# Projection and modulation units issued in four parts instead of two, in a hybrid recurrent decoder step

## The reference

```python
hmix = (_rms(x, p['norm1_w']) * (1 + sc1) + sh1)
proj = (h @ p['w_in']).astype(jnp.float32)          # q, k, v, gates of four mixers
# A gated DeltaNet, B HGRN2, C Mamba-2 SSD, D mLSTM, each 256 wide, recurrent in chunks
up = jnp.einsum('btnw,nwd->btnd', branches, p['w_branch'])
merged = jnp.einsum('btnd,btnd->btd', gates, up)
x = x + gt1 * (merged @ p['w_out'])
x = x + gt2 * _swiglu(hffn, p['ffn_w_in'], p['ffn_w_out'])
```

## Time and profile before

| | before |
|---|---|
| median of 3 runs | 1434.14 us (1432.4 to 1435.74) |
| the profiled execution | 1436.71 us, its span 1434.9 us |
| TensorE matmul busy | 1337.7 us, 93% of the span |
| VectorE busy | 633.8 us, 44% |
| ScalarE busy | 382.3 us, 27% |
| mean granted TensorE clock | 0.96 |

### The profile page before, as it was taken

The page is one execution under the profiler, slowest core; times in us unless marked ns, Lnnn a source line. Parts: engine busy times, 40 slices in busy tenths (PEclk is TensorE's granted clock), DMA queues, the critical chain, the costliest instruction groups (busy, mean ns, idle before and its releaser), DMA issues. The chain is left out here.

```text
span 1434.9 us, 23172 instructions
## 1 busy us (share of the span) xinstructions
PE 1337.7 (93%) x9801; PEld 1159.4 (81%) x9801; DVE 633.8 (44%) x1240; ACT 382.3 (27%) x561; POOL 11.7 (1%) x29
## 2 busy tenths in 40 slices
PE   6789989988999999999899999996999999989997
PEld 3368857767767676758899999896999999989996
DVE  1142663357677777463433333545322222263332
ACT  1231271173222121114521212112322222251112
POOL 0000110000000000000000000000000000000000
PEclk9889999999999999869999999998999999999999
DMA  8701703222202020305463332222233333223301
GB/s 293 219 3 59 150 12 100 68 89 89 86 4 89 1 89 1 90 0 130 49 187 98 93 84 93 74 59 60 59 88 88 88 88 88 60 60 91 88 26 63
DMA packets 191019, 116.77 MB, mean 81 GB/s; under 512 B 36650, under 2 KB 189351, under 8 KB 190678
## 3 DMA queue, kind: packets, MB, share of 16 engines
q1 hardware_dynamic: 190358, 115.41, 29.0%
q0 software_dynamic: 576, 0.14, 0.1%
HBM read 108.57 MB, written 6.96 MB: 81 GB/s over the span
## 5 line engine op out<-in xcount | busy, mean ns | idle before, releaser
L703 PE MATMUL ps<-scr_parts 128*128 128x272 f32 x2688 | 521.6, 293 | 16.7 <-DVE hT_parts L2207 8.8
L703 PEld LDWEIGHTS ps<-scr_parts 128*128 128x128 f32 x2688 | 428.8, 190 | 21.0 <-issue 13.3
L703 PE MATMUL ps<-hT_parts,scr_parts 128*128 128x272 f32 x1408 | 390.9, 291 | 0.0
L2109 DVE TENSOR_TENSOR scr_parts<-ring,scr_parts 128x1024 fp32r<-128x1024 f32 (+1 forms) x100 | 128.9, 1289 | 307.5 <-ACT scr_parts L1427 304.7
L703 PEld LDWEIGHTS ps<-hT_parts,scr_parts 128*128 128x128 f32 x1408 | 261.6, 190 | 0.0
L703 PE MATMUL ps<-hT,ring 128*128 128x272 f32 x960 | 247.6, 412 | 0.0
L1427 ACT ACTIVATE scr_parts<-ring 128x1024 fp32r<-128x1024 f32 (+1 forms) x100 | 111.1, 1112 | 491.1 <-PE ps L703 486.4
L703 PEld LDWEIGHTS ps<-hT,ring 128*128 128x128 f32 x960 | 185.7, 199 | 41.2 <-issue 3.3
L703 PE MATMUL ps<-pj_parts,scr_parts 128*128 128x272 f32 x992 | 169.2, 295 | 5.7 <-DVEq L1554 5.7
L703 PEld LDWEIGHTS ps<-pj_parts,scr_parts 128*128 128x128 f32 x992 | 143.2, 192 | 7.3 <-DVEq L1554 6.3
L703 PE MATMUL ps<-scr 128*128 128x128 f32 (+11 forms) x1288 | 136.9, 296 | 12.1 <-DVEq L1554 7.4
(11 more groups left out here) (304 smaller groups left out, 1071.0 us busy)
## 6 DMA issues: line engine op xcount, KB each, us to landing
ring<-in_w_in_dram SPq DMA_DIRECT2D x62, 512.0 KB, 6.4
ring<-in_ada_w_dram SPq DMA_DIRECT2D x48, 512.0 KB, 5.4
ring<-in_ffn_w_in_dram SPq DMA_DIRECT2D x44, 512.0 KB, 4.7
ring<-in_ffn_w_out_dram SPq DMA_DIRECT2D x16, 384.0 KB, 3.6
ring<-in_ffn_w_out_dram SPq DMA_DIRECT2D x16, 320.0 KB, 4.1
ring<-in_w_out_dram SPq DMA_DIRECT2D x8, 512.0 KB, 5.3
x_scratch<-scr SPq DMA_DIRECT2D x1, 2176.0 KB, 11.6
Q<-x_scratch SPq DMA_DIRECT2D x1, 2176.0 KB, 10.8
```

Source lines behind the costliest of these rows:

```text
L703: return pe.matmul(out, lhsT, rhs, start=start, stop=stop, skip_group_check=True)
L2109: dve.tensor_tensor(lo, src, hi.bitcast(F32), SUB).then_inc(w_split, 1)
```

## The change

A unit is divided into four parts. A part of a `mix` unit is 2 matmuls of the k loop instead of 4; a part of an `ada` unit is 4 matmuls instead of 8; a `turn` unit still does its transposes in its last part. The planner's cost of a part is halved with it. No instruction is added or removed on any engine: only the order that `shared_order` writes is another.

```diff
+PARTS = 4
@@
         elif c == "x":
-            free[eng] = start + {"mix": 1.85, "ada": 3.4, "turn": 0.3}[SEQUENCE[t][0]]
-            if part_ == 1:
+            free[eng] = start + {"mix": 0.93, "ada": 1.7, "turn": 0.15}[SEQUENCE[t][0]]
+            if part_ == PARTS - 1:
                 evac.append((free[eng], unit))
                 unit, part_ = unit + 1, 0
             else:
-                part_ = 1
+                part_ += 1
@@
-            def ada_rows_of(out, slot):
+            def ada_rows_of(out, slot, k0=0, k1=KD):
-                for k in range(KD):
+                for k in range(k0, k1):
                     last = mm(out, cT[:, k, :], ring[:, slot, k * 256:(k + 1) * 256], k == 0, k == KD - 1)
@@
-                    for k in range(4 * part_, 4 * part_ + 4):
+                    for k in range(2 * part_, 2 * part_ + 2):
@@
-                    n = load_of[("ada2", 2 * v + part_)]
-                    landed(pe, n % R, n)
-                    last = ada_rows_of(ps[0:NB + 1, u % 2, part_ * 256:(part_ + 1) * 256], n % R)
-                elif part_ == 1:
+                    e, k0 = part_ // 2, part_ % 2 * 4
+                    n = load_of[("ada2", 2 * v + e)]
+                    if k0 == 0:
+                        landed(pe, n % R, n)
+                    last = ada_rows_of(ps[0:NB + 1, u % 2, e * 256:(e + 1) * 256], n % R, k0, k0 + 4)
+                elif part_ == PARTS - 1:
@@
-                if part_ == 1:
+                if part_ == PARTS - 1:
                     last.then_inc(x_done, 1)
```

## The result

| | before | after |
|---|---|---|
| median | 1434.19 us | 1466.97 us (1465.57 to 1467.97) |
| the profiled execution's span | 1434.9 us | 1465.9 us |
| mean granted TensorE clock | 0.96 | 0.949 |

The account below looks back on a forecast made before the run. TensorE was taken to bound the kernel, through its work, idle time and low clock. Terms 3.0 + 1.5 + 3.5 + 1.0 - 5.3 gave +3.7 us, 1437.8 us on the median; range 1427 to 1447 us.

Parts of the forecast that it names:

- term e: End of the chains: parts between state stages bring back clock, -5.3 us, between -11.6 and +1.
- term a: The four hops from m_den to m_tok, tiles 0 to 4: TensorE waits longer for VectorE, +3.0 us.
- The excess hid what the planner mis-costs: Gaps along the chains: parts of 1.97 us outlast gaps planned too short; parts of 0.98 us leave half the excess.
- as late as now: Hops from m_den to m_tok: VectorE takes up m_denc no sooner than before; waits 12.9 us, or +6.4.
- b: ScalarE at the log-sigmoid passes: TensorE waits 5.5 us against 4.0, +1.5, bounds -2.5 and +4.
- c: Other hops, such as g_y to the next g_x: too little work between stages, +3.5 us, bounds 0 and +7.
- d: Clock in the tight stretch, 484 to 560 us: more waits cost clock, +1.0 us, between 0 and +5.
- the third: Rival: the early stretch falls to clock 0.91, a to c near upper bounds; about 1451 us, chance 0.14.
- The rule of the Trainium skill: Early stretch, 197 to 284 us: frequent small idle times between matmul groups would make the clock go back and forth.
- The first rival: Parts keep the clock up at the end of the chains, term e near its bound: -7, 1427 us, chance 0.28.

Follow-up runs that it names:

- the fastest kernel: The kernel before (two parts), with planner costs from the trace for m_denc, VectorE's state stages of tile 4, ScalarE's passes and h_silu: 1406.59 us, ratio 0.9797.

## Why the prediction was wrong

The side was right, the size wrong by 29 us, and the time far outside the range. The main step that failed is term e, with term a behind it. By its own terms:

- **a, forecast +3.0, measured +9.1 of waits.** "The excess hid what the planner mis-costs" is borne out by the plans with `m_denc` at 4.6 us, as far as a plan goes; the pair with a short `m_denc` says that the greater part of the loss came by other places of the order. TensorE's work between `m_den` and `m_tok` was counted well: 10.9 us forecast, the four hops (6.7, 5.5, 8.1 and 7.5 us) less their waits (16.2 with 0.50 inside the last) have 11.6. The hops were mis-sized. I took "as late as now" for the worst, 23.9 us in all as in the earlier trace rows, and they came to 27.8: in tiles 3 and 4 other chains' stages stood ahead of `m_denc` in VectorE's queue for some 3 us. Hop less 4.6 us gives 2.6, 1.7, 1.0 and 0.1 us of lateness before and 2.1, 0.9, 3.5 and 2.9 after. That the chains moved closer and queue behind each other would explain it, but is not shown.
- **b, +1.5, measured +2.0.** The first two waits were forecast at 3.2 and 2.3 us and took 3.77 and 2.58; a third of 0.99, behind one more table load, was not foreseen, and neither was its counterpart of 1.29 before. This term was right.
- **c, +3.5, measured +0.7.** My count of hops with too little work between them gave 3.8 - 1.7 - 0.9 = +1.2; the rest, for queueing, was not there.
- **d, +1.0, measured about +6.** By length times (1 - clock), 324 to 597 us lost 12.1 us before and 18.6 now, some of it inside the pauses. I had added the clock as a small term of its own. It hangs on term a: behind each of three waits of 4 us stand 2.5 to 3 us of lost clock, and behind the pause 1.8. The earlier trace rows had it: 1.11 us for four transposes behind the wait of 2.33.
- **e, -5.3, measured about +14.** This was the step that decided. Its bound "+1 (clock stays low, as before)" was wrong: if the clock stays low, the parts that the change puts into that stretch run at half level too. From 596 to 657 the loss is 0.42 x 61 = 25.6 us; before, 597 to 663 had lost 15.5 + 1.4, so +8.7, and with the waits for VectorE's run (2.04 and 4.34) +5.2. The 4.02 us wait of term a had brought the clock down before the end began: with the same order and a wait of 1.19 us (the short `m_denc`), the same stretch lost 0.29 x 53.3 = 15.5 us instead of 25.6, with 6.7 us idle instead of 6.4. But 15.5 us is what the end had lost before, too. Parts between the state stages didn't hold the clock by themselves, neither there nor in the fastest kernel, whose end lost 13.4; so even without that wait the -5.3 would not have come.
- **Not in the prediction: the pause, +4.9.** The change moved `s_out` of tile 4 from 413 to 367 us, beside three weight loads. I had looked at what the moved stages wait for, not at what else runs at their new place.

The terms as measured come to more than the 31.8 us (about 37), since clock lost in idle time costs nothing and is counted in d and e.

Of the rivals, the third (more gaps, less clock, 1451 us) was the nearest in kind, but not in its place: the early stretch that it priced kept its 1.00. The rule of the Trainium skill that stood beside it (TensorE: Matmul & The Clock Gate, A second HAM failure mode: psum-queue depth-cycling) isn't what happened: the early stretch has 0.5 us of idle time and full clock, and in the tight stretch the falls stand behind a few long waits. The first rival's mechanism is seen in the fastest kernel in part, and not in this one.

What stays open: what starts the pause (1.33 to 1.67 us without loads, none in other orders), what path the loads act on, why the same wait of 3.77 us left the clock up in one execution and not in three, and by which places of the order the false cost of `m_denc` did most of its harm. With a stock of parts that must last, I can't say that four parts are worse in principle: no run had both full cover up to 560 us and parts left at the end.

## What to carry to other kernels

When a planner fills gaps with pieces of work, the length of a piece can hide its wrong costs; before the pieces are made smaller, set the costs of the stages around them from the trace, which here was worth 27.6 us by itself, while smaller pieces with the wrong costs lost 32.8. A filler is also a stock: what it saves early is missing at the end. Price a wait with the clock that it takes down and with the work that then runs at half speed, and where a stage of many tiny matmuls is moved, look in the new trace for a pause in it that no semaphore ends.

## What the hardware showed that I had not expected

- TensorE can stop without a semaphore inside a run of 128 records of 64x4: 4.91 us with the DMA engines at 330 GB/s and 1.33 us with them at 4 GB/s in the same order, 1.67 us at 4 GB/s in another, and not at all in a third with them at 332 GB/s.
- Four waits for VectorE of 3.7 to 4 us were each followed by about 4 us or more of work at a granted clock of 0.50. One wait of 3.77 us for ScalarE was followed by full clock in one execution and by 2 us at 0.50 in three others, in the same order.
- The clock can fall while TensorE is busy without a break: in the fastest kernel it was busy for 8.00 us from 572 to 580, on records of 64x4 for most of it, with a mean clock of 0.81 in the first 4 us and of 0.50 in the next.
- Between 596 and 657 us of the changed kernel TensorE was busy for 54.62 of 61 us, and all work up to about 654 but some 2 us at 620 ran at half level.
